# A fused three-layer block whose mixture-of-experts stage gathers its input rows by index, and sums the last two experts' results on chip

## The chip, the cores and the metric

The program runs on one core of one Trainium2 chip, as one launch. The metric is the device time in microseconds (us), the median of three timed runs; a profiled execution, recorded once, supplies all the rows below. Engine names are those of the profile: PE is TensorE (PEld its weight loads), DVE is VectorE, ACT is ScalarE, POOL is GpSimd, SP is SyncE, which issues most weight loads. A "q" behind an engine name (SPq) is its instruction queue.

## The reference, cut to what matters

512 tokens of width 1024 pass a differential attention layer, an MLA layer, a third layer with dilated attention and a convolution, and then a mixture of experts. All is float32. Only the last part and the final norm are touched by the change:

```
h2 = rms_norm(x, g_norm2) * (1 + sc2) + sh2
group  = argmax(h2 @ w_rg + b_rg)                  # 1 of 4
top 2 of the 8 experts of that group               # 512 x 2 = 1024 rows in all
out[token] += weight * (silu(row @ w_gate[e]) * (row @ w_up[e])) @ w_down[e]
x = x + gt2 * out
return rms_norm(x, g_final)
```

Each expert has three float32 matrices of 2 MB (1024 x 512, 1024 x 512, 512 x 1024), and there are 32 experts, so about 200 MB of weights are read once. How many rows each expert gets depends on the data. With the inputs that the reference draws, the largest expert has 103 rows, the smallest 4, and no expert has more than its place holds (next section); of the 1024 rows, the first two experts that are worked on hold 21 and 11, and the other thirty 992.

## The kernel before, in words

Dense layers come first and fill the time to about 1080 us; the change leaves their work as it is, but for a fill of DRAM with zeros that runs beside the first attention.

**Routing** (`route`, DVE, small chained operations). It ranks the experts by their number of rows. Rank r has a fixed place of `ROWS_OF[r]` rows: ranks 0 to 2 (experts 0 to 2, always) 64 rows, ranks 3 to 9 128 rows, 10 to 16 64 rows, 17 to 31 32 rows, 2016 rows in all. Rows beyond a place would go to "further items", which run in a loop of `n_pairs` turns; here `n_pairs` is 0. `dest` holds for each token and choice the row where it goes.

**Rows.** `xs` ("expert_rows") is a DRAM tensor of all places, filled with zeros early. POOL scatters the normed tokens to it by eight indirect DMAs of 128 rows of 4 KB (L1454), waits for them, and then loads each item's whole place, padding included, by one direct DMA per item (`load_rows`, L1461) into one of two buffers `xg`. Item 0 doesn't wait for this: PE picks its rows by a product with a 0/1 matrix (`pick_rows`).

**Items** (`items`, `Plan`). One item is one expert. Their order is fixed: the ranks 0, 1, 2, then seven groups of a big one (128 rows), a narrow one (32), a middle one (64) and a narrow one, then the last narrow one: 32 items, n = 0 to 31. Item 29 is a middle one, 30 and 31 are narrow (ranks 30 and 31). In an item PE does gate and up (L1006), transposes ("flips") the next item's rows (L977), transposes the hidden values (L1036), and does the down product (L1016). ACT takes Silu (L1374) and copies (L1379). DVE multiplies (`swiglu`, L2076), scales the flipped rows (`flip`, L2066, L2069), and moves the result out of PSUM with the gate gt2 (`gated_results`, L2085). ACT's queue stores it to `ys` ("expert_results", L1383).

**Weights.** SP issues three 2 MB loads an item into a ring of three items (`load_expert`, L508). Gate and up of item n wait until gate and up of item n-3 are done; down waits for its down. So an item's loads start while the two before it are still to be worked on.

**The end.** When all results are stored, POOL gathers them by token, eight indirect DMAs of 128 rows (L1481). DVE adds them, weighted, to `x` (`add_results`, L2117), ACT squares (L1395), POOL makes the rstd of each tile of 128 tokens (L1409 to L1419), DVE applies the final norm (`last_norm`, L2123), SP stores (L546).

## Time and profile before

| | |
|---|---|
| median of 3 runs | 1653.33 us (1652.55 to 1653.66) |
| the profiled execution's own time | 1656.97 us |
| its span, first to last instruction | 1655.2 us |
| mean granted TensorE clock | 0.936 |
| PE busy | 1424.4 us (86%) |
| DVE, ACT, POOL busy | 644.3, 357.5, 103.5 us |
| HBM read, written | 323.60 MB, 32.24 MB |

The span is what the views divide. An average over the whole program says PE bounds it, and it does in the dense layers; the stage of the experts is read by itself. Times in the rows are us from the span's start. In `--windows` style rows PEclk is the share of full TensorE clock that was granted, DMA the mean busy share of the 16 DMA engines. In timeline rows the brackets tell how long the engine was idle before and what ended that. "x16" counts the merged instructions; one float32 product is recorded as two.

### The profile page before, as it was taken

Reading aid. Unit: us, or ns where it says so; the run is one execution under the profiler, and the core shown is the slowest. Engines: PE = TensorE matmul, PEld = TensorE weight load, DVE = VectorE, ACT = ScalarE, POOL = GpSimd, SP = SyncE. Lnnn points to the kernel's source line nnn. Section 1 sums busy time; section 2 is a strip of 40 time slices with the busy share of each in tenths; the row PEclk is TensorE's granted clock in tenths of the full one; section 3 lists DMA queues with packets and bytes.
Section 4 is the critical chain, followed back from the end, with each engine's and each line's share of the span. In section 5 each row is a group of like instructions: output and inputs, shape, how many; then the busy total and the mean of one; then the engine's idle time right before and its main releaser. Section 6 shows DMA issues by size and latency. Waiting matters only on the chain.

```text
span 1655.2 us, 17036 instructions
## 1 busy us (share of the span) xinstructions
PE 1424.4 (86%) x6498; PEld 724.4 (44%) x6498; DVE 644.3 (39%) x1170; ACT 357.5 (22%) x778; POOL 103.5 (6%) x236
## 2 busy tenths in 40 slices
PE   4999999889899999999899989969986876968770
PEld 2544444554455444664654456424432333423330
DVE  4664102994357413322489763242211111111113
ACT  2434002762311143431400163100000000000001
POOL 3000000010100000001100000120000000000004
PEclk9999999999999899999899989979998989979985
DMA  9762224920267431002424123269999999999984
GB/s 341 272 212 81 97 102 158 313 61 1 92 230 236 154 135 69 1 1 102 155 74 152 51 102 153 76 230 395 413 400 409 407 406 401 417 401 412 401 360 156
DMA packets 101339, 356.98 MB, mean 216 GB/s; under 512 B 9448, under 2 KB 15641, under 8 KB 92681
## 3 DMA queue, kind: packets, MB, share of 16 engines
q1 hardware_dynamic: 82512, 305.15, 48.5%
q0 software_dynamic: 9728, 34.47, 6.2%
q10 hardware_dynamic: 9016, 16.25, 2.7%
q8 instruction: 54, 0.88, 0.2%
q14 instruction: 29, 0.23, 0.0%
HBM read 323.60 MB, written 32.24 MB: 215 GB/s over the span
## 4 chain that ended last, share of the span: by engine, by line
PE 64%; DMA 17%; DVE 11%; ACT 2%; issue 2%; SPq 1%; POOL 1%; ACTq 0%; DVEq 0%; POOLq 0%
PE bank L625 15%; DMA slots<-in_w_exp_up 12%; PE score_banks L617 11%; PE score_banks L1006 9%; PE score_banks L625 9%; DVE bufD L1976 5%; PE bank L601 4%; PE bank L1016 4%; DMA slots<-in_w_exp_gate 2%; PE bank L859 2%; PE score_banks L795 2%; PE score_banks L852 2%; DMA slots<-in_ada_w 2%; PE bank L799 2%; SPq L508 1%
## 5 line engine op out<-in xcount | busy, mean ns | idle before, releaser
L625 PE MATMUL bank<-slots 128*128 128x512 f32 x608 | 265.8, 595 | 4.4 <-ACTq L1182 2.5
L617 PE MATMUL score_banks<-slots 128*128 128x512 f32 (+1 forms) x584 | 249.3, 586 | 11.4 <-ACTq L1108 6.2
L1006 PE MATMUL score_banks<-slots,norm_row 128*64 128x512 f32 (+1 forms) x768 | 174.4, 631 | 54.8 <-DMA slots<-in_w_exp_up 47.4
L625 PEld LDWEIGHTS bank<-slots 128*128 128x128 f32 x608 | 114.4, 191 | 146.7 <-issue 143.4
L617 PEld LDWEIGHTS score_banks<-slots 128*128 128x128 f32 x584 | 114.2, 198 | 139.6 <-issue 129.8
L625 PE MATMUL score_banks<-slots 128*128 128x512 f32 (+1 forms) x384 | 157.3, 570 | 0.6 <-PE bank L625 0.3
L2076 DVE TENSOR_TENSOR mix<-probsT,score_banks 128x256 f32<-128x256 f32 (+1 forms) x39 | 14.4, 370 | 326.6 <-ACT probsT L1374 326.6
L1006 PEld LDWEIGHTS score_banks<-slots,norm_row 128*64 128x64 f32 (+1 forms) x768 | 60.3, 148 | 162.9 <-issue 162.8
L1016 PE MATMUL bank<-slots,mix 128*64 128x512 f32 (+1 forms) x864 | 115.2, 477 | 11.5 <-issue 10.4
L1374 ACT ACTIVATE probsT<-score_banks 128x256 f32<-128x256 f32 (+1 forms) x39 | 13.4, 343 | 464.2 <-PE score_banks L1006 464.2
L625 PEld LDWEIGHTS score_banks<-slots 128*128 128x128 f32 x384 | 74.5, 200 | 77.7 <-issue 77.7
L1006 PE MATMUL score_banks<-slots,mix 128*32 128x256 f32 (+1 forms) x960 | 77.7, 451 | 31.1 <-issue 29.4
L1976 DVE SCALAR_TENSOR_TENSOR bufD<-slots,col,bufD 128x512 f32<-128x512 f32 x120 | 80.5, 746 | 0.4
L1016 PEld LDWEIGHTS bank<-slots,mix 128*64 128x64 f32 (+1 forms) x864 | 45.0, 121 | 66.1 <-issue 60.8
L1006 PEld LDWEIGHTS score_banks<-slots,mix 128*32 128x32 f32 (+1 forms) x960 | 39.7, 127 | 73.2 <-issue 60.7
L1637 DVE SCALAR_TENSOR_TENSOR bufD<-slots,silu_c,bufD 128x512 f32<-128x512 f32 x91 | 68.4, 752 | 4.1 <-DMA slots<-in_w_mod 0.6
L1711 DVE TENSOR_TENSOR mix<-bank,gate_row 128x512 f32<-128x512 f32 x24 | 16.6, 692 | 119.9 <-PE bank L625 119.7
L1821 DVE TENSOR_REDUCE negmax<-score_banks 128x2 f32<-128x1024 f32 x32 | 39.0, 1221 | 61.3 <-PE score_banks L795 60.6
L1637 DVE SCALAR_TENSOR_TENSOR slots<-slots,silu_c 128x512 f32<-128x512 f32 x70 | 52.6, 752 | 11.3 <-DMA slots<-in_w_mod 5.8
L1409 POOL TENSOR_SCALAR pw<-ss 128x1 f32<-128x1 f32 (+2 forms) x27 | 8.1, 299 | 768.0 <-ACT slots L1096 439.7
L601 PE MATMUL bank<-k_sb,slots 128*128 128x128 f32 x312 | 48.0, 297 | 8.0 <-ACTq L1107 3.8
L601 PEld LDWEIGHTS bank<-k_sb,slots 128*128 128x128 f32 x312 | 36.7, 150 | 32.1 <-issue 19.5
(295 smaller groups left out, 1480.9 us busy)
## 6 DMA issues: line engine op xcount, KB each, us to landing
slots<-in_w_exp_down SPq DMA_DIRECT2D x32, 2048.0 KB, 36.1
slots<-in_w_exp_gate SPq DMA_DIRECT2D x32, 2048.0 KB, 30.4
slots<-in_w_exp_up SPq DMA_DIRECT2D x32, 2048.0 KB, 32.7
slots<-in_w_in SPq DMA_DIRECT2D x16, 2048.0 KB, 8.6
slots<-in_w_mod SPq DMA_DIRECT2D x24, 1024.0 KB, 5.2
slots<-in_ada_w SPq DMA_DIRECT2D x18, 1024.0 KB, 7.2
expert_rows<-norm_row POOLq DMA_DIRECT2D x1, 12672.0 KB, 50.4
slots<-in_w_out SPq DMA_DIRECT2D x6, 2048.0 KB, 7.9
```

The lines of the kernel that those rows point to most:

```text
L601: last = nc.tensor.transpose(bank[:, i * P:(i + 1) * P], piece, ident)
L617: last = mm(bank[:, cols], w[:, k, lo:lo + P], src[:, k, cols], start=(k == 0), stop=(k == kts - 1))
L625: last = mm(bank[:, 0:cols], src[:, k, t * P:(t + 1) * P], rhs(k), start=(k == 0), stop=(k == kts - 1))
L795: return mm(bank[:, :], A8[r, h, t * P:(t + 1) * P], B8[r, h, :], start=True, stop=True)
L799: last = mm(bank[:, 0:P], pT[:, j * P:(j + 1) * P], C_tok[:, j, h * P:(h + 1) * P], start=(j == 0), stop=(j == TT - 1))
L852: mm(bank[:, :], hT[:, 2 * pair + c, t * P:(t + 1) * P], A8[:, 2 * pair + c, :], start=True, stop=False)
L859: last = mm(bank[:, c * P:(c + 1) * P], pT[:, j * P:(j + 1) * P], C_tok[:, j, h * P:(h + 1) * P], start=(j == 0), stop=(j == TT - 1))
L1006: last = mm(out, rows[:, k, :], e_gu[it.p][:, :, k, c * pc.ff:(c + 1) * pc.ff], start=(k == 0), stop=(k == KT - 1))
L1016: last = mm(psum[6 + pc.bank][c * pc.size:(c + 1) * pc.size, 0:pc.cols], hTe[pc.bank][:, lo:lo + pc.size], e_down[it.p][:, f, c * pc.cols: ...
L1637: return v.scalar_tensor_tensor(out=acc, in0=w, scalar=c, in1=acc, op0=ALU.mult, op1=ALU.add)
L1821: v.tensor_reduce(negmax[:, 2 * i:2 * i + 2], pair, AX.X, ALU.max, negate=True).then_inc(max_ready, 1)
L1976: conv_at[j] = steps(v.scalar_tensor_tensor(out=conv[:, j, :], in0=src, scalar=wcol, in1=conv[:, j, :], op0=ALU.mult, op1=ALU.add))
```

## The change

Four things are done differently.

1. `xs` becomes the normed tokens in their own order, 512 rows, stored by one SP DMA. What POOL scatters is now a table of slots, 16 bytes for a row: the token's number as an integer, the same twice as floats, and the token's weight. The table is filled beforehand with entries whose number is far out of range. ACT's queue loads the table, and `load_rows` becomes an indirect DMA that takes each row of a place from `xs` by the number in its slot; entries out of range are left out (`bounds_check`, `oob_is_err=False`), and the buffers are zeroed once so that such rows hold finite values. The fill of 3168 rows of `xs` with zeros is gone.
2. The gather of the results is issued when the items up to 29 are stored, before the last two are worked on; DVE adds tokens' tiles 0 and 1 before `swiglu` of item 31 and tiles 2 and 3 behind it.
3. The results of items 30 and 31 are not stored. DVE builds for each a matrix of weights, one row a slot and one column a token (`selection`), and PE multiplies it with the results (`sums`, eight products each, float32, 64 rows deep, 128x512 out, alternately on the lower and the upper 64 rows); DVE adds each product to `x` (`add_sum`).
4. The token weights are worked out earlier in `route`, and the last rstd are made for two tiles at a time.

```diff
-                    gp.indirect_dma_start(xs[:, :], bass.IndirectOffsetOnAxis(ap=dest[:, k, t:t + 1], axis=0),
-                                          C_tok[:, t, :], None).then_inc(rows_out, 16)
-            pool.wait_ge(rows_out, 16 * 2 * TT)
+                    gp.indirect_dma_start(table[:, :], bass.IndirectOffsetOnAxis(ap=dest[:, k, t:t + 1], axis=0),
+                                          own_slot[:, k * TT + t, :], None).then_inc(slots_out, 16)
+            gp.memset(bufD[:, 1792:2048], 0.0).then_inc(rows_zeroed, 1)
+            pool.wait_ge(rows_zeroed, 2)
+            pool.wait_ge(xs_out, 16)
+            pool.wait_ge(first_slots_in, 16)
             def load_rows(it, unrolled=True):
...
-                gp.dma_start(xg[it.q][0:it.rows], xs[bass.ds(it.first, it.rows), :]).then_inc(xg_in[it.q], 16)
+                gp.indirect_dma_start(xg[it.q][0:it.rows], None, xs[:, :],
+                                      bass.IndirectOffsetOnAxis(ap=it.row_ids[0:it.rows, 0:1].bitcast(I32), axis=0),
+                                      bounds_check=T - 1, oob_is_err=False).then_inc(xg_in[it.q], 16)
...
             for it in items[1:]:
                 load_rows(it)
+            pool.wait_ge(zeros_out, 16)
+            for n in range(5):
+                pool.wait_ge(y_out[n], 16 * (P // (NARROW if n > 2 else WIDE)) * plan.stores[n])
...
+                    gp.indirect_dma_start(gathered[k][:, t, :], None, ys[:, :],
+                                          bass.IndirectOffsetOnAxis(ap=dest[:, k, t:t + 1], axis=0)).then_inc(gath[t], 16)
```

In SP's queue and in PE's program (the wait of `sums` for `results_taken` is left out here):

```diff
+            sp.wait_ge(xn_ready, 4 * TT)
+            sp.dma_start(xs.rearrange("(t p) d -> p t d", p=P), C_tok).then_inc(xs_out, 16)
             sp.wait_ge(logitsT_ready, 2)
             load_ahead(2, 1)
             sp.wait_ge(rows_picked, 1)
-            sp.wait_ge(rows_out, 16 * 2 * TT)
+            sp.wait_ge(xs_out, 16)
             load_ahead(2, 2)
...
+            def sum_up(pieces, j, bank, done):
+                t, half = j % SUMS // 2, j % 2
+                r = slice(half * WIDE, (half + 1) * WIDE)
+                for pc in pieces:
+                    last = mm(bank[:, :], pc.select[t // 2][r, t % 2 * P:(t % 2 + 1) * P], y_buf[pc.buffer][r, :],
+                              start=pc is pieces[0], stop=pc is pieces[-1])
```

On DVE the end of the items' stage stood so before (names: `sinT` holds the gate for narrow items, `slots` the gathered results, `wts` the token weights; the first row is item 30's result):

```order
L2085 TENSOR_TENSOR bufD<-bank,sinT 128x256 [waits y_stored4,down_done_b]
L2076 TENSOR_TENSOR mix<-probsT,score_banks 128x128 [waits silu_gate_ready_a,h_transposed_a]
L2085 TENSOR_TENSOR bufD<-bank,sinT 128x256 [waits y_stored3,down_done_a]
L2107 TENSOR_LOAD inv_sums
```

and stands so now (`sums` holds the slots' words, the token weights among them):

```order
L2231 TENSOR_TENSOR bufD<-bank,slots 128x512 [waits y_stored1,down_done_b]
L2245 TENSOR_TENSOR x<-score_banks,x 128x512 [waits results_summed]
L2245 TENSOR_TENSOR x<-bank,x 128x512 [waits results_summed] x2
L2251 SCALAR_TENSOR_TENSOR x<-slots,sums,x 128x1024 [waits results_gathered0,results_taken]
L2251 SCALAR_TENSOR_TENSOR x<-slots,sums,x 128x1024 [waits dve_step,results_gathered1]
L2216 TENSOR_TENSOR mix<-probsT,score_banks 128x128 [waits dve_step,silu_gate_ready_a,h_transposed_a]
L2251 SCALAR_TENSOR_TENSOR x<-slots,sums,x 128x1024 [waits results_gathered2]
L2251 SCALAR_TENSOR_TENSOR x<-slots,sums,x 128x1024 [waits dve_step,results_gathered3]
L2231 TENSOR_TENSOR bufD<-bank,slots 128x512 [waits dve_step,y_stored2,down_done_a]
```

Between item 30's result and item 31's, where one multiplication stood, there are now eight additions of sums and eight additions of gathered rows, four of these ahead of the multiplication.

On PE the same place, between item 30's down product (`bank<-slots,mix`) and item 31's gate and up, shows the eight products of `sums`:

```order
L1072 MATMUL bank<-slots,mix 32x256 [waits y_ready_b,h_transposed_copied_b,expert_down_loaded0]
L1081 MATMUL score_banks<-bufD,probsT 128x512 [waits y_ready_b,selection_ready]
L1081 MATMUL bank<-bufD,probsT 128x512 x2
L1081 MATMUL score_banks<-bufD,probsT 128x512 [waits results_taken]
L1062 MATMUL score_banks<-slots,norm_row 32x256 [waits rowsT_ready,h_ready_a,expert_up_loaded1,expert_gate_loaded1]
```

Eight more stand at PE's end, behind item 31. In `route` on DVE nine small operations now stand between the masks' sums and the first use of the counts (`bank,k_sb 32x32`):

```order
L1682 CAST sums<-k_sb 128x8
L1683 COPY sums<-k_sb 128x8
L1684 TENSOR_SCALAR sums<-k_sb 128x8
L1687 TENSOR_REDUCE bufD<-bufD 128x4 [waits router_exp_out]
```

The six from `TENSOR_REDUCE` on stood behind the routing before.

## Rows read from the trace of the kernel before

**Rows 1.** Part 2 of the page: 40 slices of the span, busy tenths.

```profile
PE   4999999889899999999899989969986876968770
...
DMA  9762224920267431002424123269999999999984
```

**Rows 2.** DMA queues of the stretch 1118 to 1608: packets, MB, share of 16 engines.

```profile
q1 hardware_dynamic: 23707, 182.61, 92.0%
q10 hardware_dynamic: 6528, 8.13, 4.6%
q0 software_dynamic: 2374, 7.72, 4.6%
...
slots<-in_w_exp_up SPq DMA_DIRECT2D x29, 2048.0 KB, 32.8
...
expert_results<-bufD ACTq DMA_DIRECT2D x48, 128.0 KB, 7.9
bufD<-expert_rows POOLq DMA_DIRECT2D x7, 512.0 KB, 10.8
bufD<-expert_rows POOLq DMA_DIRECT2D x15, 128.0 KB, 7.0
```

**Rows 3.** The chain of waits, one group of four items.

```profile
1439.03 35.46 DMA slots<-in_w_exp_up
```

**Rows 4.** Stretches: PE, PEld, DVE, ACT, POOL busy (instructions), PEclk, DMA share, GB/s.

```profile
1090.00:1098.00 8.00, 1.72 (x10) 0.93 (x9) 5.55 (x24) 1.40 (x3) 0.63 (x1) 0.50 0.00 0
...
1592.00:1596.00 4.00, 4.00 (x52) 2.56 (x48) 0.00 (x0) 0.00 (x0) 0.00 (x0) 0.62 1.04 431
...
1608.00:1612.00 4.00, 4.00 (x44) 2.24 (x40) 0.00 (x0) 0.00 (x0) 0.00 (x0) 0.50 0.27 110
```

**Rows 5.** Timeline, routing to item 1: start, us, engine, line, what [idle before].

```profile
1089.93 0.19 ACT L1367 ACTIVATE bufD<-bufD 128x4 f32<-128x4 f32 x1
...
1090.70 0.18 DVE L1551 SCALAR_TENSOR_TENSOR bufD<-bank,k_sb 32x32 f32<-32x32 f32 x1 [0.86 <-PE bank L960]
...
1106.45 0.95 POOL L1454 DMA_INDIRECT expert_rows<-slots,dest  x1 [0.30 <-issue]
...
1111.49 1.12 POOL L1461 DMA_DIRECT2D bufD<-expert_rows  x2 [4.08 <-DMA expert_rows<-slots,dest]
...
1119.12 1.07 PE L977 MATMUL score_banks<-k_sb,bufD 64*128 64x64 f32 x8 [0.75 <-DMA bufD<-expert_rows]
```

**Rows 6.** Timeline, end of the items.

```profile
1588.53 1.14 ACTq L1383 DMA_DIRECT2D expert_results<-bufD  x2
...
1600.44 0.42 DVE L2085 TENSOR_TENSOR bufD<-bank,sinT 128x256 f32<-128x256 f32 x1 [1.68 <-PE bank L1016]
...
1607.11 6.11 PE L1006 MATMUL score_banks<-slots,norm_row 128*32 128x256 f32 x64 [6.72 <-issue]
...
1613.66 0.29 DVE L2076 TENSOR_TENSOR mix<-probsT,score_banks 128x128 f32<-128x128 f32 x1 [12.79 <-ACT probsT L1374]
...
1630.16 5.36 DVE L2117 SCALAR_TENSOR_TENSOR x<-slots,wts,x 128x1024 f32<-128x1024 f32 x4 [13.00 <-DMA slots<-expert_results,dest]
...
1646.72 0.92 POOL L1409 TENSOR_SCALAR pw<-ss 128x1 f32<-128x1 f32 x1 [0.45 <-ACT slots L1395]
...
1649.40 1.28 DVE L2123 SCALAR_TENSOR_TENSOR slots<-x,ss,gate_row 128x1024 f32<-128x1024 f32 x1 [1.80 <-POOL ss L1419]
```

**Rows 7.** Timeline: item 7's row load and its flip, the shortest distance.

```profile
1177.48 0.56 POOL L1461 DMA_DIRECT2D bufD<-expert_rows  x1 [11.51 <-PE score_banks L977]
...
1195.95 1.16 PE L977 MATMUL score_banks<-k_sb,bufD 128*128 128x128 f32 x8
```

**Rows 8.** Timeline: a full-width product, and a narrow one after a pause.

```profile
1056.94 7.03 PE L625 MATMUL bank<-slots 128*128 128x512 f32 x16
...
1567.84 3.66 PE L1006 MATMUL score_banks<-slots,mix 128*32 128x256 f32 x64
...
1591.44 5.35 PE L1006 MATMUL score_banks<-slots,mix 128*32 128x256 f32 x64 [3.67 <-issue]
```

More of the change, by code:

```diff
@@ L2082, in gated_results @@
                     dve.wait_ge(down_done[pc.bank], pc.used + 1)
-                    if not unrolled or pc.stores:
-                        dve.wait_ge(y_out[pc.buffer], 16 * pc.tiles * pc.stores)
-                    v.tensor_tensor(y_buf[pc.buffer][:, 0:pc.cols], psum[6 + pc.bank][:, 0:pc.cols], gates[pc.size], ALU.mult)\
-                        .then_inc(y_ready[pc.bank], 1)
-            def items_in_turn(items, unrolled=True):
-                for it, after in zip(items, items[1:]):
-                    swiglu(it, unrolled)
-                    flip(after, it)
-                    gated_results(it, unrolled)
@@ L2094, in _ @@
-            gates = {WIDE: cosT[:, :], NARROW: sinT[:, 0:256]}
-            dve.wait_ge(rows_picked, 1)
-            v.tensor_copy(xg[0][:, 0:W], psum[4][:, :]).then_inc(picked_copied, 1)
-            flip(items[0])
+                    if unrolled and pc.stores:
+                        dve.wait_ge(y_out[pc.buffer], 16 * pc.tiles_stored * pc.stores)
+                    if pc.slots is None or pc.size == WIDE:
+                        v.tensor_tensor(y_buf[pc.buffer][:, 0:pc.cols], psum[6 + pc.bank][:, 0:pc.cols], gates[pc.size], ALU.mult)\
+                            .then_inc(y_ready[pc.bank], 1)
+                        continue
@@ new lines, in add_sum, with add_results @@
+            def add_sum(j, bank, done, taken, n):
+                t, cols = place_of_sum(j)
+                dve.wait_ge(done, n + 1)
+                v.tensor_tensor(x[:, t, cols], bank[:, :], x[:, t, cols], ALU.add).then_inc(taken, 1)
+            def add_results(t):
+                dve.wait_ge(gath[t], 32)
+                for k in range(2):
+                    chain(v.scalar_tensor_tensor(out=x[:, t, :], in0=gathered[k][:, t, :], scalar=own_slot[:, k * TT + t, 3:4],
+                                                 in1=x[:, t, :], op0=ALU.mult, op1=ALU.add))
+                dve.sem_inc(results_added, 1)
```

300 lines of the change are left out of this document (223 added, 77 removed).

## The prediction, made before the changed kernel was run

> **What bounds the kernel now.** I read the slices first [rows 1]: PE is near full up to slice 27, and from slice 26 on, where the items begin, the DMA engines stand at 9 in every slice and PE falls to 6 to 9. So the dense part is PE's and the items' part is DMA's. The chain of waits says the same: one group of four items is a piece of 35.46 us of waiting for `w_exp_up` and then PE's product [rows 3]. The queues of the stretch from 1118 to 1608 [rows 2] show what the 490 us are made of: q1 (SP's weights) 182.61 MB at 92.0% of 16 engines, q10 (ACT's stores) 8.13 MB at 4.6%, q0 (POOL's row loads) 7.72 MB at 4.6%. Shares sum to about 101%, so a byte taken out is time taken out, and one put in is time put in. Last the timeline of the end [rows 6]: item 31's gate and up start at 1607.11, when its weights have come; from there to the span's end 48.1 us pass, and in them all weights are already there. That end is made of the item, its stores, a gather, additions and the norm, one behind the other.
>
> I call W the time at which item 31's gate and up start: 1607.1 before. The sum has two parts, what moves W, and what follows it.
>
> **What moves W.**
>
> Start of the stream. Nine DVE operations are put ahead of the counts. DVE idled 0.86 us there for PE [rows 5]; the exponentials are ready at 1090.12, so the three copies hide and the six others, about 0.2 us each as their small neighbours take, run from 1090.1 to 1091.4, plus 0.3 for their chaining, against 1090.70: +1.0 us. It delays `dest`, `pick_rows` and the end of item 0's gate and up, whose freed buffer starts the first load of the stream. The scatters still take 1.25 us each to issue, last at 1106.45+1.0, but then 16 bytes a row land where 4 KB did. Behind them stand a table load by ACT and one indirect load, so item 1's rows can land about 1118.5 where they landed at 1119 for a flip at 1119.12 [rows 5]. PE comes to that flip at about 1119.4 now, so the +1.0 covers it. Should the table's round trip be 3 us longer, PE waits 2 to 3 us once. The new 2 MB store of the normed tokens lies ahead of the stretch 1090 to 1098, in which no DMA engine works [rows 4]: nothing. If that were full, 5 us. The zero fill that goes runs beside the first attention, PE-bound [rows 1]: nothing gained.
>
> Rows. q0 took 4.6% of 490 us, 22.5 us, for 1888 rows of items 2 to 31. Of these 992 are real. If rows out of range move nothing, 896/1888 of 22.5 us go: -10.7 us. No row shows an out-of-range index. The bounds are 0 (they move as before) and -10.7; I take -10.7, since the text of the change zeroes the buffers once, which is needed only if such rows aren't written.
>
> Stores. Item 30's 32 rows leave the stream: 32/1984 of q10's 22.5 us, -0.4 us. Item 31's store lay in the end.
>
> The gather. 1024 rows of 4 KB at q0's rate of 22.5 us for 1888 are 12.2 us of all engines, now inside the stream. It starts when item 29's stores have landed: issued at 1588.5 and 1589.1, 7.9 us each to landing [rows 6, 2], 1597; shifted by +1.0 and -10.7, about 1587.5, first bytes about 1589.5. Without the gather W would be 1607.1+1.0-10.7-0.4 = 1597.0, so 7.5 us of weights are still to come. Bounds: the gather waits behind them, W = 1597.0; or goes ahead of them all, W = 1609.2. Which is it? POOL's 128 KB loads land in 7.0 us and its 512 KB loads in 10.8, while a weight load takes 32.8 [rows 2]: POOL's queue doesn't wait behind the backlog of weights, and its extra 384 KB took 3.8 us, about 100 GB/s of some 406, a quarter. The packets say the same: q1's are 7.7 KB, q0's 3.25 KB, so turns packet by packet give q0 30%. At 30% the 7.5 us of weights become 10.7: W = 1600.2. The gather then has the engines nearly to itself, and all traffic, item 31's down among it, ends 2.1 us later than before. Before, the engines ran out between 1608 and 1612 [rows 4]; so the last gathered tile lands at about 1612.5.
>
> The Trainium skill ("DMA: Bandwidth & Descriptors", Queues, rings and completion order) says that each DMA engine takes its queues in turn, packet by packet. The landing times above agree with that.
>
> **What follows W.** Item 30's result is ready at 1600.86-9.7, 1591.2. `sums(0)`, eight products, ends by about 1600.5, in PE's idle time before item 31 (6.72 us before, [rows 6]); DVE's eight additions at 0.7 us (a result of half that width takes 0.42, [rows 6]) end at 1601.3, and tiles 0 and 1 are added by about 1607, as they land. If weights came earlier than 1600.5, `sums(0)` would hold PE; if the gather is late, DVE, which works in order, holds item 31's `swiglu`. So item 31's hidden values are ready at about 1607.5 and its down by 1611. Tile 2 is added meanwhile, tile 3 waits for its rows at 1612.5: two additions of 1.3 us (four took 5.36, [rows 6]), done 1615.2. Item 31's result stands behind it on DVE, 0.7 us: 1615.9. Who waits is PE with `sums(1)`.
>
> `sums(1)`: a full-width product over 512 columns is 7.03/8 = 0.88 us [rows 8]. PE has paused about 5 us; after a pause of 3.67 us the clock was 0.62 for the next 4 us and the narrow product took 5.35 where it takes 3.66; after 6.72 us it took 6.11 [rows 8, 4, 6]. So 7.0+2.1 = 9.1 us. The bounds are 7.0 and, all at 1.2 GHz, 14.1. DVE adds 0.7 us each, hidden but the last. Then: 0.1+9.1+0.8 = 10.0 for the sums; ACT's square of the last tile 1.3; POOL's six operations from 1646.72 to 1649.36, 2.65; two final norms of 1.3, since the last rstd now serves two tiles, 2.6; and the 4.5 us from the last norm's end (1649.40+1.28) to the span's end. That is 21.1, and 1615.9+21.1 = 1637.0.
>
> The register loads of `n_pairs` on DVE and PE now stand ahead of the last sums. SP's pause between an item's last load and the next one's first, which holds such a load, is never under 2.3 us nor shown alone; so 0 to 2.3 us, and I take 0, since PE's falls in its pause and DVE's beside the first product. The moved gather itself saves nothing on DVE: the eight additions remain.
>
> **The sum.** Against its own execution, span 1655.2: 1637.0-1655.2 = -18.2 us. In its terms: W -6.9, and 48.1 us behind W become 36.8, of which some wait for the gather. The profiled execution took 1656.97, 3.6 above the median of the runs; I take the difference over to the median: 1653.3-18.2 = 1635.1, predicted 1635.
>
> **The rivals.**
> - Padding still moves. POOL has to write a descriptor for each row, and could write one to nowhere; for it speaks that nothing shows otherwise. Then all behind the stream lies 10.7 us later: 1645.8.
> - The gather goes ahead of the weights (W = 1609.2). Then the way from W is 6.55 us to `swiglu`'s start, 0.3, four additions 5.4, the result 0.7 and 21.1, 34.1 in all: span 1643.3, time 1641.4. Against it speaks POOL's quarter above.
> - Pairs of sums run side by side, as alternate products use the lower and the upper 64 rows. Column halves do so: narrow outputs cost less per product. Then DVE's additions, 0.75 us each, bound `sums(1)`: 6.0 instead of 9.1 and the result is 1632. The Trainium skill ("TensorEngine Tiling (Array Packing)", Key Properties) says that different tiles can execute in parallel; no row here has row halves alone.
> - Slower than before: an indirect load of rows lands later than its flip. A direct one has 18.5 us from issue to flip at its tightest (1177.48 to 1195.95, [rows 7]) and lands in 7 to 10.8. Below 18.5 us it costs nothing. Above that PE waits at each big item, and as buffers are freed later the DMA engines run dry. At 22 us: seven groups by 3.5 us, 24.5 more, and 1635+24.5 = 1659.6, slower; the turn lies at 2.6 us a group, so at a landing of about 21 us. Against it: the scatters, indirect too, took about 4 us to land.
> - The change doesn't do what it says: a place whose rows exceed it would take the further items' loop. None does.
>
> **How the numbers follow.** Forecast 0.50; padding moves 0.18; gather first 0.12; side by side 0.07; slower rival 0.13. The forecast's own range is 1630 to 1643 (14.1 for the sums would add 5, an early gather take 2.5). Padding together with a slow clock reaches 1651. The range 1627 to 1652 leaves out the slower rival and little else. This kernel's measurement tells 0.2%, 3.3 us, from no change: faster is below 1650.0. All cases but the slower rival are faster in the main, less a part of padding's: faster 0.83, same 0.05, slower 0.12.
>
> **What would show it.** Right: q0 in the stream with about 4 MB of rows beside the gather's 4.2; the flips never waiting for rows; item 31's gate and up at about 1600, with PE busy on sums just before; the last gather landing near 1612 and the last additions ending near 1615; eight products in about 9 us. Wrong: q0 with 7.7 MB of rows; W near 1609 or beyond; PE idle before the flips, waiting for a row load; products of sums at 0.44 or 1.75 us each; a DVE gap over 2 us behind item 31's result.

## The result, and the profile after

| | before | after |
|---|---|---|
| median, same chip | 1653.49 us (1652.55 to 1654.09, 4 runs) | 1629.27 us (1627.20 to 1630.65, 4 runs) |
| ratio after to before, 95% interval | | 0.9854 (0.984 to 0.9868) |
| the profiled execution's own time | 1656.97 us | 1630.65 us |
| its span | 1655.2 us | 1628.9 us |

The change takes 24.2 us off, 1.5%. The forecast was 1635, the range 1627 to 1652. The time lies at the range's fast end, and the parts don't have the sizes that the prediction gave them.

I keep one ledger for every kernel below. The **stream** runs from SP's gate load of item 3, the first load of the stream, to W, where item 31's gate and up start; the **tail** from W to the span's end.

| profiled executions, us | first load | W | stream | tail | span |
|---|---|---|---|---|---|
| before | 1118.6 | 1607.1 | 488.5 | 48.1 | 1655.2 |
| after | 1117.9 | 1591.9 | 474.0 | 37.0 | 1628.9 |
| difference | -0.7 | -15.2 | -14.5 | -11.1 | -26.3 |

The span's 26.3 are 2.1 more than the medians' 24.2, since the profiled execution of before lay 3.5 above the median of the table and that of after 1.4 above its own.

The slices of after, part 2 of the page:

```profile
PE   4999999889999999999899989968997868879784
...
DMA  9762323400167624002243221347999999999994
```

It is still PE's program until about slice 27, and the DMA engines' from there on [rows 1]. The queues of after, stretch 1118 to 1590 (packets, MB, share of 16 engines), the counterpart of [rows 2]:

```profile
q1 hardware_dynamic: 23463, 181.66, 93.4%
q10 hardware_dynamic: 6336, 8.00, 4.7%
q0 software_dynamic: 2387, 4.37, 2.7%
...
bufD<-normed_rows,w_router POOLq DMA_INDIRECT x29, 6.9
```

POOL's queue carries 4.37 MB (its rows and the gather's first bytes) where it carried 7.72, and an indirect load of rows lands in 6.9 us. SP's queue moves its 181.66 MB in 93.4% of 472 us, 412 GB/s while it is at it; before it was 182.61 MB in 92.0% of 490 us, 405 GB/s. So besides the rows that are gone, the weights themselves came 1.7% faster.

The start of the routing's new part and of the rows, timeline of after (start, us, engine, line, what), beside [rows 5]:

```profile
1087.69 0.18 DVE L1699 SCALAR_TENSOR_TENSOR bufD<-bank,k_sb 32x32 f32<-32x32 f32 x1
...
1103.78 0.96 POOL L1567 DMA_INDIRECT expert_slots<-sums,dest  x1 [0.30 <-issue]
...
1112.32 0.98 POOL L1581 DMA_INDIRECT bufD<-normed_rows,w_router  x1 [7.25 <-DMA w_router<-expert_slots]
...
1117.62 1.09 PE L1033 MATMUL score_banks<-k_sb,bufD 64*128 64x64 f32 x8
```

The last row is item 1's flip (the transposes of its rows), with no idle time before it: its rows were there. For all flips of the items' stage the trace names nothing but issue, 15.1 us over 31 times, as what ended PE's idle time before them (durations in ns, first and last start, forms):

```profile
L1033 PE MATMUL score_banks<-k_sb,bufD x248: 269/270/376, 1117.6 to 1580.5; 32*128 32x32 f32 x60, 64*128 64x64 f32 x36, 128*128 128x128 f32 x28
its engine sat idle before it (us, times) until:
  issue: 15.1, 31
```

And now the end, timeline of after, beside [rows 6]. First POOL and PE:

```profile
1584.57 0.66 PE L1081 MATMUL score_banks<-bufD,probsT 64*128 64x512 f32 x1 [0.90 <-DVE bufD L2231]
...
1585.81 0.95 POOL L1606 DMA_INDIRECT slots<-expert_results,dest  x1 [25.10 <-DMA expert_results<-bufD]
...
1591.89 4.23 PE L1062 MATMUL score_banks<-slots,norm_row 128*32 128x256 f32 x47 [1.82 <-issue]
...
1604.84 0.48 PE L1114 MATMUL bank<-k_sb,mix 128*128 128x128 f32 x1 [6.56 <-DVE mix L2216]
...
1611.07 2.98 PE L1081 MATMUL score_banks<-bufD,sinT 64*128 64x512 f32 x8 [2.06 <-DVE bufD L2231]
1613.78 2.71 PE L1081 MATMUL score_banks<-bufD,w_router_scaled 64*128 64x512 f32 x8
```

Then DVE:

```profile
1596.46 2.60 DVE L2251 SCALAR_TENSOR_TENSOR x<-slots,sums,x 128x1024 f32<-128x1024 f32 x2 [5.66 <-issue]
...
1601.67 2.60 DVE L2251 SCALAR_TENSOR_TENSOR x<-slots,sums,x 128x1024 f32<-128x1024 f32 x2 [2.61 <-DMA slots<-expert_results,dest]
...
1604.50 0.29 DVE L2216 TENSOR_TENSOR mix<-probsT,score_banks 128x128 f32<-128x128 f32 x1 [0.22 <-DVE x L2251]
1604.70 5.35 DVE L2251 SCALAR_TENSOR_TENSOR x<-slots,sums,x 128x1024 f32<-128x1024 f32 x4
1610.28 0.69 DVE L2231 TENSOR_TENSOR bufD<-bank,slots 128x512 f32<-128x512 f32 x1 [0.22 <-DVE x L2251]
...
1615.61 2.72 DVE L2245 TENSOR_TENSOR x<-score_banks,x 128x512 f32<-128x512 f32 x4 [0.30 <-PE score_banks L1081]
...
1623.03 2.48 DVE L2310 SCALAR_TENSOR_TENSOR slots<-x,ss,gate_row 128x1024 f32<-128x1024 f32 x2 [1.69 <-POOL ss L1528]
```

Read the second fence from the bottom up. The last norms follow ACT and POOL, these the last addition, which ends at 1618.33. From 1601.67 to there DVE is idle for 2.5 us in all, 2.1 of them waiting for PE's last products: the end now belongs to DVE and to the gathered rows that it waits for, and PE waits for it (6.56 us before item 31's transposes). The chain of waits that ended last agrees: it goes from item 29's stores over the gather to DVE, and the weights aren't in it any more; between item 31's result and DVE's last additions it holds the first six of PE's last eight products. Some of its pieces (start, us, what):

```profile
1574.91 9.93 DMA expert_results<-bufD
...
1589.55 12.10 DMA slots<-expert_results,dest
1601.67 1.29 DVE x L2251
...
1611.07 4.56 PE score_banks L1081 x12
```

### The profile page after: what moved, and what is told of

Read it like the earlier page. It is cut to its first block, busy times and chain, and to the rows that moved or that the text cites. A ratio compares the mean times of both kernels' runs of the same rounds, so it can differ in the third digit from the quotient of the medians.

```text
span 1628.9 us, 17192 instructions
## 1 busy us (share of the span) xinstructions
PE 1431.7 (88%) x6530; PEld 727.9 (45%) x6530; DVE 659.3 (40%) x1202; ACT 357.1 (22%) x778; POOL 111.0 (7%) x228
## 4 chain that ended last, share of the span: by engine, by line
PE 67%; DMA 16%; DVE 12%; ACT 2%; issue 2%; SPq 1%; POOL 0%; DVEq 0%; ACTq 0%; POOLq 0%
PE bank L681 15%; DMA slots<-in_w_exp_up 12%; PE score_banks L673 11%; PE score_banks L1062 10%; PE score_banks L681 9%; DVE bufD L2116 5%; PE bank L1072 4%; PE bank L657 4%; PE bank L915 2%; PE score_banks L851 2%; PE score_banks L908 2%; DMA slots<-in_ada_w 2%; PE bank L855 2%; DVE bufD L1777 1%; PE score_banks L911 1%
## 5 line engine op out<-in xcount | busy, mean ns | idle before, releaser
L673 PE MATMUL score_banks<-slots 128*128 128x512 f32 (+1 forms) x584 | 247.5, 583 | 11.4 <-ACTq L1198 6.1
L1062 PE MATMUL score_banks<-slots,mix 128*32 128x256 f32 (+1 forms) x960 | 77.2, 446 | 25.4 <-issue 22.3
L1518 POOL TENSOR_SCALAR pw<-ss 128x1 f32<-128x1 f32 (+3 forms) x25 | 7.5, 300 | 787.1 <-ACT slots L1186 436.8
L1581 POOL DMA_INDIRECT bufD<-normed_rows,w_router x31 | 30.4, 979 | 425.3 <-PE score_banks L1033 417.7
```

The lines of the kernel that those rows point to most:

```text
L673: last = mm(bank[:, cols], w[:, k, lo:lo + P], src[:, k, cols], start=(k == 0), stop=(k == kts - 1))
L1062: last = mm(out, rows[:, k, :], e_gu[it.p][:, :, k, c * pc.ff:(c + 1) * pc.ff], start=(k == 0), stop=(k == KT - 1))
```

## The experiments

Theory A is the prediction's own: 896 rows out of range move nothing, worth the 10.7 us that their queue's share of the engines says; the early gather costs the weights some of it; products of sums take 0.88 us each; the rest of the gain is the end's new order. The rivals: the padding still moves; the gather costs the weights nothing or everything; products run two at a time. The first four kernels were timed on one chip, where before took 1654.1 (median of 13 runs, 1649.03 to 1657.61). Of kernels that ran once the ledger is read instead: the stream repeats within 1.5 us where nothing in it was changed (473.6 to 475.1 over after and five other kernels), while the start of the routing scatters over 7 us (1076.4 to 1083.5) and is left out of the comparisons. W is the time at which PE starts, and that is held by the weights or, where the sums of item 30 run late, by PE itself; where it matters I also give the landing of item 31's up, the last of the two matrices that W needs.

**1. The empty slots point to real rows again.**

```diff
-            gp.memset(fill[:, :, SLOT - 1], 0.0).then_inc(fill_ready, 1)
+            steps(gp.memset(fill[:, :, SLOT - 1], 0.0))
+            for n in range(fill.shape[1]):
+                steps(gp.memset(fill[:, n:n + 1, 0].bitcast(I32), 15 * n))
...
```

> The changed kernel, but the empty slots of the table hold the numbers of real tokens (33 different ones) and a weight of 0, so every padding row is moved again: 896 rows in items 2 to 31. Result unchanged. Theory A, a padding row costs what POOL's queue shows for it (22.5 us of engines for 1888 rows): 10.7 us more, 1640 us. Rival B, padding rows also slow the packets of the weights, as the weights' own rate rose from 405 to 412 GB/s between the two traces: about 17 us more, 1646. In both q0 shows 7.7 MB in the stream beside the gather; by B the weights' rate falls back to 405 GB/s.

Measured 1645.60 (9 runs), ratio to before 0.9944 (0.9929 to 0.9959): the rival's 1646, not theory A's 1640. W 1611.2, stream 488.5, tail 35.1. The weights' rate is 405 GB/s again (queues of the stretch 1123 to 1609):

```profile
q1 hardware_dynamic: 23301, 181.06, 91.9%
q0 software_dynamic: 2395, 7.90, 4.6%
```

So the gain in the stream is the 896 rows that don't move; fetching by index, which both kernels have, costs it nothing that shows. The size is less sharp than the equal 488.5 suggests: here PE is busy with the sums of item 30 right up to W, and the last landing of item 31's up that the trace holds (some records are missing) is at 1609.5, 1.8 us before W. The rows are worth 12.9 to 14.5 us by this pair.

A slot that is left out isn't wholly nothing. POOL's queue has about as many packets in after as before (2387 and 2374 in the two tables of queues). Between 1130 and 1570, 873 of them carry 4 KB in after and 1278 carry 4 bytes; before, it was 1668 and 447. A packet of 4 bytes takes 9 ns (median), one of 4 KB 159 to 161.

**2. The rows by index alone**, the gather and all results at the end as before.

```diff
-                    if late < 0:
+                    if True:
...
-                if it is items[-1]:
-                    sums(0)
...
-                if unrolled and it.n < EXPERTS - LATE_ITEMS:
+                if unrolled:
...
-            sums(1)
```

> The first part of the change alone: table of slots, rows gathered by number, token weights early; all items stored, gather, additions and norms at the end as before. Theory A: 1 us later start, 11 us less in the stream: 1653.5 - 10 = 1643.5 us. Rival B: 16 to 17 us less in the stream: 1637 to 1638 us. The time from item 31's gate and up to the end stays 48 us in both.

Measured 1640.07 (5 runs), ratio 0.9925 (0.9901 to 0.9949); stream 473.6, tail 48.7. The time lies between the two expectations, and its interval has room for both, so the ledger has to decide. PE is idle ahead of W in before and here (6.72 and 6.58 us), so in both W is the weights' own, and the stream is shorter by 14.9 us: the rows alone give it the whole of its gain, and more than theory A's 11. They leave the tail about as long as it was (48.1). After against this kernel has a tail shorter by 11.7 and a time shorter by 10.8.

**3. The gather waits for the last weights.**

```diff
+            for j in range(3):
+                pool.wait_ge(e_in[items[-1].p][j], 16 * items[-1].loads)
             for n in range(5):
                 pool.wait_ge(y_out[n], 16 * (P // (NARROW if n > 2 else WIDE)) * plan.stores[n])
```

> The changed kernel, but the gather of the results also waits until the three matrices of item 31 have landed, so it shares no time with weights. Theory A, the gather took about 30% of the engines for the 6 us in which both ran, and weights are late by 2 us for it: W (item 31's gate and up) 2 us earlier, the gather starts 9 to 10 us later and all behind it, 1636 to 1638 us. Rival: the early gather only pushes the weights back by its whole size, so that nothing is gained by it: W 12 us earlier and 1629 us in all.

Measured 1637.29 (4 runs), ratio 0.990 (0.987 to 0.993). The gather is issued at 1597.25 instead of 1585.81, and the tail is 42.4 instead of 37.0: of the 11.7 us between `rows_only` and after the early gather is 5.4. The other 6.3, the results summed on chip and the rstd in pairs, no run takes apart. The time is in theory A's range, but the 2 us that W was to gain aren't there: item 31's up lands 474.0 us behind the first load here (1591.3) and 473.9 in after (1591.8). The early gather delays item 31's gate and up by nothing. Where does its room come from? The stretches of this kernel before its W of 1591.4 (columns as in [rows 4]):

```profile
1586.00:1588.00 2.00, 2.00 (x7) 0.80 (x8) 1.01 (x2) 0.00 (x0) 0.00 (x0) 1.00 0.55 233
1588.00:1590.00 2.00, 2.00 (x7) 0.91 (x7) 1.98 (x4) 0.00 (x0) 0.00 (x0) 1.00 0.42 176
1590.00:1592.00 2.00, 1.95 (x17) 0.79 (x18) 1.98 (x4) 0.00 (x0) 0.00 (x0) 1.00 0.44 182
```

and the same stretches of after:

```profile
1586.00:1588.00 2.00, 2.00 (x7) 0.88 (x6) 1.98 (x4) 0.00 (x0) 1.70 (x2) 1.00 0.70 262
1588.00:1590.00 2.00, 2.00 (x7) 0.59 (x4) 1.98 (x4) 0.00 (x0) 1.39 (x3) 1.00 0.88 326
1590.00:1592.00 2.00, 0.18 (x5) 0.14 (x8) 0.80 (x2) 0.00 (x0) 1.42 (x2) 0.86 1.01 387
```

In its last 6 us the weights' stream leaves about half of the engines' time empty (share 0.55 to 0.42). Each load lands in 16 parts, and the trace has their times one by one. Of item 31's down nine parts land here between 1580.2 and 1588.7 and the other seven between 1593.5 and 1596.3; from 1588 to 1593 seven or eight packets of SP's queue are in flight at a time, where it was 13 to 15 around 1580. So some engines have run dry while others still have weights queued, and the gather works in the former: 0.70, 0.88, 1.01.

This room is new with the change. Before, the parts of item 31's up landed within 6.3 us of each other, and the share was still 0.84 at 1605 to 1607, just before W. In `rows_only` they land 17.0 us apart, and in after and this kernel about as far; that distance grows over the stream, from about 2 us in its first items. Leaving out the empty slots thus seems to load the engines unevenly, and W waits for the slowest. How much earlier W would come with even engines wasn't tested.

What the gather does delay is the last load, item 31's down: its last part lands 479.0 us behind the first load here (1596.3) and 483.6 in after (1601.5). That is 4.6 us, and in after it is hidden behind DVE. POOL's row in this kernel, the wait for that load:

```profile
1597.25 0.96 POOL L1608 DMA_INDIRECT slots<-expert_results,dest  x1 [36.99 <-DMA slots<-in_w_exp_down]
```

**4. The zero fill put back.**

```diff
+            old_rows = scratch.rearrange("(p m) d -> p m d", p=FILL_P)
+            gp.dma_start(old_rows, norm_row[0:FILL_P, :].unsqueeze(1).to_broadcast([FILL_P, old_rows.shape[1], D])).then_inc(scratch_out, 16)
```

> The changed kernel plus the old fill of 12.7 MB with zeros, into a DRAM tensor that nothing reads, issued where it was. Theory A, the fill was hidden beside the first attention: no difference, 1629 us. Rival: the 3.7 us that the dense part is shorter in the changed kernel's trace come from the missing fill: 1633 us, and the routing starts about 3.7 us later.

Measured 1633.71 (4 runs), ratio 0.9871 (0.984 to 0.9902), 4.4 us over after, 2.8 by the ratios, with intervals that overlap. Its stream (474.7) and tail (38.0) are nearly those of after; what is longer is the dense part, where routing starts at 1082.4 against 1078.7. That is what the rival expected, 1633 and 3.7 us later. But kernels without the fill started it anywhere between 1076.4 and 1083.5, so this doesn't show that the fill costs something. It stays unclear.

**5. Item 31's work ahead of the additions**, a try at a faster kernel.

```diff
+            swiglu(items[-1])
             add_results(0)
             add_results(1)
-            swiglu(items[-1])
+            gated_results(items[-1])
             add_results(2)
             add_results(3)
-            gated_results(items[-1])
```

> DVE works in order. In the changed kernel item 31's swiglu stands behind the additions of tiles 0 and 1, and its gated result behind those of tiles 2 and 3: the swiglu ran at 1604.50 although gate and up had ended near 1598, and PE stood 6.56 us before item 31's transposes. Here the swiglu stands ahead of tiles 0 and 1 and the gated result ahead of tiles 2 and 3; nothing else changes. Theory A (DVE's order holds PE, and PE's last eight products come late for it): PE's transposes of item 31 follow its gate and up within 2 us, the last eight products are spread under the additions, and DVE's last addition ends where its own work ends, about 1615.8 where it was 1618.3: -2.5 us, about 1626.7. Theory B (the last additions wait for the gathered rows or for DVE's total work, which is the same): the end stays within 0.5 us, 1629. Rival on the other side: the gated result, now ahead, waits for item 31's down while tiles 2 and 3 are already there, and DVE idles up to 2 us for it: 1630 to 1631.

Measured 1631.61 (4 runs, 1628.15 to 1631.77), ratio 0.9864 (0.9846 to 0.9882): no gain over after, whose interval it shares. The timeline, PE:

```profile
1596.42 0.33 PE L1114 MATMUL bank<-k_sb,mix 128*128 128x128 f32 x1 [0.81 <-DVE mix L2216]
1599.94 2.92 PE L1072 MATMUL bank<-slots,mix 128*32 128x256 f32 x32 [3.19 <-DMA slots<-in_w_exp_down]
```

PE's 6.56 us of waiting are gone as expected, but 3.19 of them come back as a wait for the down weights, which the gather had delayed, and DVE has the same work to do. The profiled execution, the fastest of the four, took 1628.15 with the last addition ending at 1615.9, near theory A's 1626.7 and 1615.8, but its stream began 2.8 us earlier than that of after. By the ledger its last addition ends 25.6 us behind W instead of 26.4, the tail is 36.1 against 37.0. Theory B is nearer: the order is worth 0.8 us where PE had waited 6.56. PE's clock stood at 0.50 in this kernel from 1602 to 1614, so its last products ran at the lower of the two levels (1.2 GHz); what the order gives at full clock wasn't measured.

**6. Products over all 128 rows.** Each product here sums over the other half's rows too.

```diff
-                r = slice(half * WIDE, (half + 1) * WIDE)
+                r = slice(0, P)
```

> Each product that sums results uses all 128 rows of its selection and of its results in place of 64, so every sum is over both halves' rows (the sums are another quantity then); the count of products, their 512 columns and all else are unchanged. Theory A (products on the lower and the upper 64 rows run side by side in the changed kernel): here they can't, and a product takes 0.88 us at full clock against 0.50 that four of them took each in the kernel whose gather waits; the last eight take 7 us and more (10 at the lower clock that stood at that place), the last addition ends 2 to 5 us later than 1618.3, span about 1631 to 1634. Theory B (the 0.50 comes from something else, such as the rows that a product uses being few): the same time per product with 64 rows or 128 would speak against it only if four products again take 2 to 3 us; then the end stays at 1618.3.

One run: 1627.32. The span is 1625.6 and the last addition ends at 1615.37, not the 1631 to 1634 and 2 to 5 us later that were expected: the stream began 4.9 us earlier here than in after. So the last stretch has to be read by itself. What matters are the last sixteen instructions (eight products), and PE's clock in them. The timeline of this kernel, then its windows:

```profile
1605.84 5.37 PE L1081 MATMUL score_banks<-bufD,sinT 128*128 128x512 f32 x8 [2.45 <-DVE bufD L2231]
1611.05 3.60 PE L1081 MATMUL score_banks<-bufD,w_router_scaled 128*128 128x512 f32 x8
```

```profile
1609.00:1614.00 5.00, 5.00 (x12) 2.24 (x11) 3.64 (x6) 2.55 (x5) 0.64 (x2) 0.95 0.00 0
1612.00:1617.00 5.00, 2.64 (x7) 0.86 (x5) 4.17 (x6) 3.45 (x6) 1.93 (x7) 1.00 0.00 0
```

A full-depth product takes 3.60/4 = 0.90 us at a clock of 0.95 to 1.0, as [rows 8] say. From the first product to the last there are 8.81 us here and 5.42 in after (1611.07 to 1616.49), where the clock was lower, 0.65 in the first three microseconds:

```profile
1611.00:1614.00 3.00, 2.93 (x10) 1.58 (x12) 1.29 (x2) 0.31 (x1) 0.00 (x0) 0.65 0.02 5
```

At full clock, in the kernel whose gather waits, four half-depth products took 1.99 us, 0.50 each:

```profile
1616.38 1.99 PE L1081 MATMUL score_banks<-bufD,sinT 64*128 64x512 f32 x8 [1.78 <-DVE bufD L2233]
```

A product could also be cheap because it uses few rows. The sums of item 30 in after, at full clock, speak against that:

```profile
1584.57 0.66 PE L1081 MATMUL score_banks<-bufD,probsT 64*128 64x512 f32 x1 [0.90 <-DVE bufD L2231]
1584.57 0.69 PE L1081 MATMUL bank<-bufD,probsT 64*128 64x512 f32 x1
...
1588.35 1.12 PE L1081 MATMUL score_banks<-bufD,probsT 64*128 64x512 f32 x2
```

Two products, one on each half, start in the same hundredth of a microsecond, and a half-depth product takes 1.12 us from its start to its end; a full-depth one takes 1.02 (at 1585.91 in this kernel, clock 1.00). It is no quicker for its 64 rows; two share the time. So a pair on the lower and the upper 64 rows runs side by side. The Trainium skill ("TensorEngine Tiling (Array Packing)", Key Properties) says that different tiles can execute in parallel; this pair of kernels shows it for row halves, 0.50 against 0.90 us. What it is worth here is less. From item 31's result to the last addition there are 9.85 us here (1605.52 to 1615.37) and 7.36 in after, 2.5 more and so within the expectation's 2 to 5. In the 7.36 DVE adds for 5.3 us (0.65 to 0.69 each) and waits 2.1 for PE: PE's products at the lower clock set the pace first, DVE's additions at the end. The tail as a whole is only 0.9 longer (37.9 against 37.0), since the way from W to item 31's result was 1.3 shorter in this execution.

**7 to 12. What a row in the stream costs.** After experiments 1 and 2 a difference was open: the 896 rows had 10.7 us of the engines by their queue, yet are worth up to 14.5. Six kernels add about as many rows of 4 KB to the changed kernel, in POOL's queue, in six ways. First DRAM to DRAM, in large pieces and row by row, at the seven big items:

```diff
+                if it.rows > WIDE:
+                    at_row = P * (it.rank - FIXED)
+                    gp.dma_start(scratch[at_row:at_row + P, :], xs[0:P, :]).then_inc(scratch_out, 16)
```

> The changed kernel, with seven copies of 128 rows of 4 KB from DRAM to DRAM put into POOL's queue, one behind the row load of each big item: 896 rows, as many as the empty slots that no longer move, but not into the row buffers. From the first load of the stream to item 31's gate and up the kernel before took 488.5 us and the changed one 474.0, 14.5 less, where POOL's queue itself took only 11 us less of the engines. Theory A (any extra traffic of that size costs that much, own time and a slower weight stream): 488 to 489. Theory B (the extra 4 us come from writes into the row buffers beside the weights' writes): 484 to 485, that is the copies' own 11 us. Theory C (copies that write to DRAM are dearer than either): over 490. Behind the stream nothing changes: tail 37 us.

(The second kernel writes to `scratch[at_row:at_row + P, 0, :]` of a tensor twice as large.)

> As the kernel with seven copies from DRAM to DRAM, but each of the 896 rows goes to a place of its own, 8 KB apart, so that it travels as a piece of 4 KB and not within a large one. With large pieces the stream was 481.9 us, 7.9 more than the changed kernel. Theory A (what counts is the number of 4 KB pieces, not where they go): 488 to 489, as with rows into the row buffers. Theory B (the row buffers' side counts, or the bytes alone): 482 again.

Then into the row buffer, ahead of a big item's real row load:

```diff
+                if unrolled and it.rows > WIDE:
+                    gp.dma_start(xg[it.q], xs[0:P, :]).then_inc(again_in, 16)
+                    pool.wait_ge(again_in, 16 * (it.rank - FIXED + 1))
```

> The changed kernel, in which POOL loads 128 rows of 4 KB into a big item's row buffer once more ahead of its real row load, and waits for them: seven times 128, 896 rows, as many as the empty slots, but of the big items and by a direct transfer. The stream from its first load to item 31's gate and up takes 474.0 us in the changed kernel, 488.5 where the empty slots' rows move, 481.9 where 896 rows are copied DRAM to DRAM in large pieces. Theory A (rows of 4 KB into the row buffers cost 16 ns each, wherever they stand): 488 to 489. Theory B (it is the many small loads of the smaller items that cost more): 483 to 485, as the queue's own 11 us say. Rival: the second load makes the real one late for its flip (two of 7 us in a row against 18.5 us of room), then PE's flips of big items show idle time for rows and the stream is over 490.

Then into fewer partitions, in more loads, with these lines in the same place, the first for every item from 2 on with at least 64 rows, the second for every item from 2 on:

```diff
+                    gp.dma_start(xg[it.q][0:WIDE], xs[0:WIDE, :]).then_inc(again_in, 16)
...
+                    gp.dma_start(xg[it.q][0:NARROW], xs[0:NARROW, :]).then_inc(again_in, 16)
```

> The changed kernel; POOL loads 64 rows of 4 KB once more ahead of the real row load of every item with at least 64 rows from item 2 on: 15 loads, 960 rows, into partitions 0 to 63. 896 rows in loads of 128 put 8.8 us on the stream (474.0 to 482.8), and so did 896 into DRAM (483.0); the empty slots, whose rows are in the loads of 32, 64 and 128, took 14.5. Theory A (loads that write to few partitions, and more of them, cost more per row, and slow the weights beside them: their rate falls from 412 to about 405 GB/s): 960 rows add 12 to 16 us, stream 486 to 490. Theory B (a row costs 9.8 ns in a load of any size): +9.4, stream 483.4, weights at 412 GB/s.

> As the kernel with 64 rows more, but 32 rows into partitions 0 to 31, ahead of the real row load of each of items 2 to 31: 30 loads, again 960 rows. Theory A (few partitions): dearer still than with 64, stream 488 to 494, weights at 405 GB/s or under. Theory B (a row costs 9.8 ns in any load): 483.4. If both this and the kernel with 64 come out at 483, the missing 5.7 us of the empty slots' 14.5 are neither the row buffers, nor the loads' size; then they belong to how the row loads with empty slots in them stand to the weights' loads, and stay open.

And last the 64 rows again, on every second partition: `xg[it.q][0:P:2]`.

> As the kernel with 64 rows more per load (15 loads, 960 rows of 4 KB, stream 498.4 us against 474.0, weights at 403 GB/s), but the 64 rows go to every second of the 128 partitions instead of partitions 0 to 63. Rows, bytes, source, loads and waits are the same. Theory A (a block of few partitions makes the row dear): the cost falls to that of loads over all 128 partitions, 9.8 ns a row: +9.4, stream 483.4, weights at 412 GB/s. Theory B (it is the loads of fewer rows, or their same 64 source rows): as before, stream 498.

One run each, but for the last (median of nine):

| kernel | rows, loads | where to | time | stream | over 474.0 | a row | weights |
|---|---|---|---|---|---|---|---|
| dram_copies | 896, 7 | DRAM, large pieces | 1635.19 | 481.9 | 7.9 | 8.8 ns | 412 GB/s |
| dram_rows | 896, 7 | DRAM, 4 KB pieces | 1640.92 | 483.0 | 9.0 | 10.0 ns | 412 |
| rows_twice | 896, 7 | partitions 0 to 127 | 1634.77 | 482.8 | 8.8 | 9.8 ns | 413 |
| rows64_again | 960, 15 | partitions 0 to 63 | 1655.43 | 498.4 | 24.4 | 25.4 ns | 403 |
| rows32_again | 960, 30 | partitions 0 to 31 | 1657.63 | 502.8 | 28.8 | 30.0 ns | 398 |
| rows64_spread | 960, 15 | every second of 128 | 1640.67 | 482.7 | 8.7 | 9.1 ns | 412 |
| padding_moves | 896 empty slots | as the places | 1645.60 | 488.5 | 14.5 | 16.2 ns | 405 |

The weights' rate is q1's bytes over q1's busy time from the first load to 6 us before W. In `rows_twice` and `padding_moves` PE's sums held W; their up landed at 481.8 and, as far as recorded, 486.8, so their excess may be 0.9 and 1.6 us smaller than the table has it. The queues of rows64_again and then of rows64_spread, 1118 to 1590:

```profile
q1 hardware_dynamic: 22399, 173.64, 91.6%
q0 software_dynamic: 3525, 7.83, 5.1%
```

```profile
q1 hardware_dynamic: 23096, 179.05, 92.0%
q0 software_dynamic: 3488, 7.74, 4.4%
```

Packets and bytes of POOL's queue are nearly the same, 3525 and 3488 packets, 7.83 and 7.74 MB. With the block of 64 partitions they take 5.1% of the engines instead of 4.4, and SP's queue gets 5.4 MB less through in the same 472 us. The last pair is the cleanest of the study: rows, bytes, source, number of loads and waits are equal, only the partitions differ, and 24.4 us become 8.7. Neither the number of loads nor the side (DRAM or row buffer) does this. Nor do late rows: PE did wait for rows ahead of flips, 5.4 us in `rows64_again` and 2.8 in `rows64_spread`, but the mean share of the engines up to 6 us before W, all queues together, is 1.01 in both, so no DMA time was lost by it. Of the difference of 15.7 us SP's queue has 11.2 (449.6 against 438.4 us of the engines) and POOL's 4.4 (25.1 against 20.7).

As to the expectations: `dram_copies` and `rows_twice` came out under every theory, `dram_rows` and `rows64_spread` within 1 us of the cheap one (482 and 483.4), and the loads into 64 and 32 partitions over every theory, 498.4 and 502.8 against at most 490 and 494.

The Trainium skill ("SBUF — State Buffer", Door 1: The DMA port swizzle) says that a transfer's bandwidth depends on how many of 16 ports its partitions reach, and its table gives partitions 0 to 63, and 0 to 31 alike, the same eight. The runs agree in both: 64 and 32 partitions are near each other (25.4 and 30.0 ns), and every second of 128, which reaches all sixteen, is as cheap as 128. They add that the weights beside such a load slow down too (403 and 398 GB/s against 412). The ports themselves no run shows; the runs show the partitions.

Of the 896 empty slots 311 stand in places of 128 rows, 291 in places of 64 and 294 in places of 32. At the measured prices of 9.8, 25.4 and 30.0 ns they would be worth 3.0+7.4+8.8 = 19.3 us; at 9.8 ns all, 8.8. Measured are 14.5 (12.9 at the least), between the two. Why not 19.3 isn't settled: a row in a load that goes to these partitions anyway may cost less than one in a load of its own, and by the landings of experiment 3 the engines run apart once the padding is gone.

## Why the prediction was right, and where it wasn't

The mechanisms were right in the main: the items' stage is the DMA engines', the data of rows out of range doesn't move, and the end shortens by the early gather. The time came out 5.7 us below the forecast, just under the narrower range of 1630 to 1643 too. Two terms failed, the price of a row and the gather's cost to the weights. Step by step:

- **Start of the stream, +1.0.** In the routing the new operations cost 2.82 us from the masks' product (1084.87) to the counts (1087.69), against 2.14 before: +0.7. Item 1's flip didn't wait for rows. The traces put the first load 0.7 earlier, less than the scatter of the dense part.
- **Rows, -10.7.** The bound that I took was right in kind and too small: -12.9 to -14.5 by experiment 1, -14.9 by experiment 2. The failed step is the reading of a row's price from its queue's share of the engines alone. That share (4.6% of 490 us) leaves out what the load does to the weights beside it: from `padding_moves` to after POOL's queue needs 10.0 us less of the engines up to 6 us before W (21.4 and 11.4), about as I had it, and SP's queue 4.9 less (443.9 and 439.0). And it had no notion of partitions.
- **Stores, -0.4.** q10 carries 8.00 MB where it carried 8.13: as said, too small to see in the time.
- **The gather, +3.2 on W.** It failed: nothing, by experiment 3. The premise "a byte put in is time put in" holds in the stream's middle, where the shares sum to 101%, and not in the last 6 us of the changed kernel, where about half of the engines' time is empty. The sharing that I described does happen, but it falls on item 31's down (4.6 us), which is hidden. The rival with the gather ahead of the weights fell with it.
- **W.** Forecast 1600.2, measured 1591.9. The 8.3 us are 1.7 of the start, 3.4 of rows and stores together (14.5 where I had 11.1) and 3.2 of the gather.
- **From W to item 31's result.** Forecast 15.7 us, measured 19.1 (1591.89 to 1610.97). DVE, in order, held the `swiglu` as the prediction said it would if the gather came late, and by more: the tiles 0 and 1 were added by 1604.27, 12.4 us behind W, where I had counted 6.8. With W so early, the gathered rows end the wait and no longer the weights.
- **From there to the end.** Forecast 21.1, measured 17.9. The sums' stretch was 7.4 us (1610.97 to 1618.33) and not 10.0: products in pairs. I had given this rival 0.07; by its numbers the stretch would be 6.9. With full-depth products, which is what I had priced, it was 9.85 (experiment 6). The smaller terms were off both ways: the square and POOL's second round took 4.7 us (1618.33 to 1623.03) where I had 3.95, the pair of norms 2.48 (2.6), and from its end to the span's end there were 3.4 us and not 4.5. The register loads cost nothing (PE starts 0.1 us behind the result).
- **The tail as a sum.** 36.8 forecast and 37.0 measured, but by two errors of about 3.3 us that cancel. The forecast was right there by luck.
- **Rivals.** Padding still moves: refuted by experiment 1, whose price for it, 1645.6, lies on the rival's 1645.8; it got there by luck, with rows that are dearer than I had them and a gather that is cheaper. Rows late for their flip: no flip waits for rows in the items' stage of after, and an indirect load lands in 6.9 us.

## What to carry to other kernels

In a stage that DMA bounds, price a small transfer by what it does to the stage, not by its share of the queues: a load into a block of 64 partitions cost nearly three times what the same rows cost on every second of 128, and 10.6 of its 24.4 us showed up as slower weights (449.6 against 439.0 us of SP's queue). Spread narrow tiles over the partitions (not tried here for the places themselves), or don't move their padding. And look at the last microseconds of a stream apart: with the empty slots left out the engines ran out up to 17 us apart, so a gather put into that gap was free for the load that mattered, and the next wait was not the stream's but that of the engine whose order I had filled up.

## What the runs showed of the hardware that was not expected

- An indirect load leaves out the data of rows whose index is out of range: 4.0 MB in place of 7.5 in POOL's queue from the first load to 6 us before W, and the stream 474.0 us in place of 488.5. A packet of 4 bytes stays in place of each row's 4 KB.
- With rows left out the 16 parts of a 2 MB load came to land 17 us apart; with all rows moved, 6.3.
- 960 more rows of 4 KB put 24.4 us on a saturated stream where they went to partitions 0 to 63, and 8.7 us where they went to every second partition.
- Copies from DRAM to DRAM cost a saturated stream 8.8 ns per 4 KB in large pieces and 10.0 in pieces of 4 KB, as much as loads over 128 partitions.
- A product 64 rows deep and 512 columns wide took 0.50 us where two such alternate on the halves, and 0.90 at full depth.
- In after PE's granted clock fell in PE's idle time before item 31's transposes, was 0.50 from 1602 to 1608, and 0.98 from 1610 to 1612. It was 0.50 again from 1612 to 1614, behind PE's 2.06 us of waiting for item 31's result. Four half-depth products took 2.98 us across that second fall and 1.99 at full clock.
